# The two parts of each head trade places by transfers instead of ScalarE copies, in the rotations of a two-block transformer kernel

## The chip, the cores and the metric

One core of one Trainium2 chip. The metric is device time in microseconds (us) of the whole program; lower is better. Engines are named as in the profile: PE is TensorE's matmul, PEld its weight load, DVE VectorE, ACT ScalarE, POOL GpSimd, SP SyncE; a name with a q (ACTq, SPq, PEq) is the engine's queue, in which waits are passed and transfers are issued.

## What is computed

The reference runs a block of depth two (two attention mixers with two MLPs) over 512 tokens of width 1024, and then a second block, where the change lies. The second block applies a rotary embedding to heads of 64 channels before its attentions:

```
def apply_rope(x, cos, sin):
    half = x.shape[-1] // 2
    xf = x.astype(jnp.float32)
    x1, x2 = xf[..., :half], xf[..., half:]
    return jnp.concatenate([x1 * cos - x2 * sin, x2 * cos + x1 * sin], axis=-1).astype(x.dtype)

dq = apply_rope(...)      # four heads of two parts: differential attention
dk = apply_rope(...)
nq = apply_rope(...)      # eight query heads: compressed, selected and window attention
k_cmp = compress(apply_rope(kv(kc_), c3, s3), cmp_pe_k, cmp_k_w1, cmp_k_w2)
k_sel = apply_rope(kv(ks_), c3, s3)
k_win = apply_rope(kv(kw_), c3, s3)
```

Everything is float32. The weights come as slabs of 512 KB.

## The kernel before

**Layout.** Channels lie on the 128 partitions, tokens along the free axis (512). A slab is 128x1024 and holds, mostly, eight 128x128 weight tiles that give one 128x512 result. Each float32 product is made from two rounded parts: ScalarE rounds a slab to `w_hi` (`split`, L1052, two halves), GpSimd makes the rest `w_lo` (L456, two halves), and TensorE runs three matmuls a tile (L481 to L483). Slabs have two buffers in each of `raw`, `w_hi` and `w_lo`: slab m+2 is split when the matmuls of slab m are done, and SyncE loads the next one into `raw` (L437) when GpSimd has finished with it.

**The stage of the change.** In the second block a plan in units called halves (`E_PLAN`) strings the projections together: q, k, v for four pairs of heads, kc and vc for the compressed keys and values, ks, vs, kw, vw, four nq, the gates, and the two compression matrices w1 (slabs of sixteen narrow tiles, matmuls L848 to L850). Beside the plan run 48 steps of attention. A step s has scores on PE (L935), maxima on DVE (L1721), exponentials on ACT (`weigh`, L1154), shares on DVE (L2143 to L2148), a scaling on ACT (L1448 or L1162), a transpose on PE (`e_flip`, L944), a copy on DVE (L2134 or L2136) and the product with the values on PE (L972 or L981). Each engine takes its instructions in the program's order; nothing is rescheduled while it runs.

**A rotation.** Fifteen results are rotated, numbered n = 1 to 15 by `E_ROPE` in the order q0, k0, kc, q1, k1, q2, k2, q3, k3, ks, nq0, kw, nq1, nq2, nq3. Each has four parts:

- `e_first` on DVE: L2070 writes the bank times the signed sine to `tmp[:, n % 2]`, L2071 writes the bank times the cosine to the destination.
- `e_swaps` on ACT (L1414): four copies of 32 partitions by 512 elements, from `tmp[:, n % 2]` to `tmp[:, 2 + n % 2]`, rows r from rows r^32. From n = 3 on, it waits first for the addition of rotation n-2 (L1411).
- `e_second` on DVE: waits for `swapped`, then adds the exchanged tile to the destination (L2027) and tells PE (`rope_ready`).
- PE waits for `rope_ready` before the first scores of a pair and before the compressed scores `cs` (L904, matmuls L907).

In step s the order on ACT is: `weigh(s)`, swaps of half 2s-1, `e_half(2s)`, the scaling of step s, swaps of half 2s, `e_half(2s+1)`. On DVE it is: maxima(s), `e_half(2s)`, the copy of step s-1, the rotation's addition of half 2s-1, shares(s), `e_half(2s+1)`, the differential combination, the addition of half 2s. `e_half` on ACT holds the splits of the slabs and small work of its own (logarithm and exponential of the sub-norm, L1399 and L1400; the copies of `windows`, L1367 and L1368; `u_hi`, L1384).

ACT's queue also issued transfers before, elsewhere: the loads of x, one store of a bias table (L1212), four table loads (L1178) and half of the stores of the result (L1527).

Of the kernel before, what the change touches and what calls it, by code (L numbers as in the profile page):

```python
# [36 lines left out]
ACT = mybir.ActivationFunctionType  # L37
# [220 lines left out]
E_ROPE = {}  # L258
# [28 lines left out]
def build(nc, slabs, x_in, params_in, consts_in, pos1_in, pos2_in, rel_in, lam_in, y_out):  # L287
    n_slabs = slabs.shape[0]
    rel_rows = nc.dram_tensor("rel_rows", (8, E_LEN), F32, kind="Internal").ap()
    with ExitStack() as stack:  # L290
# [3 lines left out]
        def sem(name):  # L294
            return stack.enter_context(nc.semaphore(name))
# [25 lines left out]
        tmp = sb("tmp", [4, S])  # L321
# [73 lines left out]
        act_hi, act_lo = sem("act_hi"), sem("act_lo")  # L395
        sq_ready, acc_ready, softened = sem("sq_ready"), sem("acc_ready"), sem("softened")
        rstd_ready, squared_rstd = sem("rstd_ready"), sem("squared_rstd")
        swapped, rope_ready = sem("swapped"), sem("rope_ready")
        dve_step, act_step = sem("dve_step"), sem("act_step")
        rel_ready, masks_ready, fox_ready = sem("rel_ready"), sem("masks_ready"), sem("fox_ready")  # L400
        t_ready, y_stored = sem("t_ready"), sem("y_stored")
# [638 lines left out]
        def _(act):  # L1040
# [363 lines left out]
            def e_swaps(h):  # L1404

                for name, p, turn in ends_of(h):
                    if name in ROTATED:
                        n = E_ROPE[name, p]
                        act.wait_ge(gemm_free, taken_out[name, p])
                        if n > 2:  # L1410
                            act.wait_ge(rope_ready, n - 2)  # L1411
                        for r in range(0, P, 32):
                            o = r ^ 32
                            last = act.activation(tmp[r:r + 32, 2 + n % 2, :], tmp[o:o + 32, n % 2, :], ACT.Copy)  # L1414
                        last.then_inc(swapped, 1)

            def e_half(h):
                for name, p, turn in ends_of(h - 2):
# [113 lines left out]
        def _(dve):  # L1532
# [489 lines left out]
            def e_second(name, p):  # L2022
                if name in ROTATED:
                    n = E_ROPE[name, p]
                    dve.wait_ge(swapped, n)
                    dst = rotated(name, p)
                    dve.tensor_tensor(dst, dst, tmp[:, 2 + n % 2, :], ALU.add).then_inc(rope_ready, 1)  # L2027
                elif name == "tk":
# [26 lines left out]
            def e_first(name, p, turn):  # L2055
# [5 lines left out]
                if name == "pct" and p >= 2:  # L2061
                    dve.wait_ge(valued, e_valued(DIFF_STEPS + 8 * (p - 1)))
                if name in ROTATED and E_ROPE[name, p] > 2:
                    dve.wait_ge(swapped, E_ROPE[name, p] - 2)
                dve.wait_ge(gemm_full, c.gemm.at(1))
                c.gemm.now += 1
                if name in ROTATED:
# [3 lines left out]
                    last = dve.scalar_tensor_tensor(rotated(name, p), bank, scale, cos2[:, :], ALU.mult, ALU.mult)  # L2071
                elif name in ("v", "vc", "vs", "vw"):
                    last = dve.tensor_tensor(VT[:, :], bank, rstd[:, :], ALU.mult)
                elif name == "ng":
                    last = dve.tensor_tensor(VT[0:24, :], bank[0:24, :], rstd[0:24, :], ALU.mult)
                elif name == "b":
                    last = dve.tensor_tensor(g_b[:, p, :], bank, rstd[:, :], ALU.mult)
                elif name == "w1":
                    last = dve.tensor_copy(hs[0:CC, :], bank[0:CC, 0:256])
# [3 lines left out]
                elif name == "gt":  # L2083
                    last = dve.tensor_copy(gates[:, :, :], bank[:, 0:NB * 24])
# [307 lines left out]
```

## Time and profile before

| | us |
|---|---|
| median of 3 runs | 2106.61 |
| lowest, highest | 2105.53, 2108.70 |
| the profiled execution, its own time | 2107.49 |
| its span in the trace | 2105.70 |
| stage of the rotations in the trace | 1276 to 1560 |

The span begins with the first recorded instruction and ends with the last; 1.79 us of the profiled execution's own time lie around it. A row of a timeline reads: start, duration, engine, line, operation, destination <- sources, shape, count, and in brackets how long the engine had been idle before, with what ended it. "PEclk" is the share of full TensorE clock that was granted.

### The profile page before, as it was taken

How to read it: one execution, taken by the hardware profiler on the slowest of the kernel's cores; microseconds unless marked ns; L12 is line 12 of the kernel's file. 1: busy time of each engine (PE TensorE's matmuls, PEld its weight loads, DVE VectorE, ACT ScalarE, POOL GpSimd, SP SyncE). 2: the span in 40 equal slices, each digit the busy share in tenths (PEclk: the TensorE clock that was granted, in tenths of full speed). 3: DMA queues.
4: the chain of work that ended last, by engine and by line, in shares of the span. 5: the costliest groups of instructions: out<-in, count | busy, mean ns of one | idle time of the engine just before them, and what ended most of it. 6: DMA issues, size and time to landing. Idle time of an engine off the chain costs nothing.

```text
span 2105.7 us, 28470 instructions
## 1 busy us (share of the span) xinstructions
PE 2037.0 (97%) x9900; PEld 1604.6 (76%) x9900; DVE 967.5 (46%) x1559; ACT 902.7 (43%) x1760; POOL 870.4 (41%) x648
## 2 busy tenths in 40 slices
PE   9999999999999988899999999999999999999997
PEld 6777688888887755688888887766667888888886
DVE  6444545322255677542312255557655653323133
ACT  5444443333343654442323346656654333223234
POOL 3222354444454221254444454442113555445454
PEclk9999999999999999999999999999999999999999
DMA  4222123223222110122223322221111222323323
GB/s 156 71 71 81 59 92 101 93 97 100 93 96 90 61 41 31 41 91 100 100 91 99 100 90 80 94 97 41 41 41 62 99 92 99 100 91 100 100 90 110
DMA packets 50581, 177.88 MB, mean 84 GB/s; under 512 B 5536, under 2 KB 5800, under 8 KB 50480
## 3 DMA queue, kind: packets, MB, share of 16 engines
q1 hardware_dynamic: 48096, 172.07, 24.7%
q10 hardware_dynamic: 2384, 4.43, 0.7%
q8 instruction: 67, 1.10, 0.2%
q14 instruction: 34, 0.28, 0.0%
HBM read 174.36 MB, written 2.12 MB: 84 GB/s over the span
## 4 chain that ended last, share of the span: by engine, by line
issue 47%; PE 31%; POOL 19%; DVE 2%; POOLq 1%; ACT 0%; DVEq 0%; ACTq 0%
POOL w_lo L456 19%; PE gemm_banks L481 9%; PE gemm_banks L482 9%; PE gemm_banks L483 9%; PE score_banks L935 1%; PE out_bank L981 1%; PE score_banks L944 1%; DVE turned L2136 1%; POOLq L450 0%; POOLq L455 0%; PE gemm_banks L907 0%; DVE score_banks L1721 0%; DVE x L2232 0%; PE out_bank L972 0%; ACT tmp L1414 0%
## 5 line engine op out<-in xcount | busy, mean ns | idle before, releaser
L456 POOL TENSOR_TENSOR w_lo<-raw,w_hi 128x512 fp32r<-128x512 f32 x644 | 870.2, 1373 | 1218.1 <-ACT w_hi L1052 1218.0
L1052 ACT ACTIVATE w_hi<-raw 128x512 fp32r<-128x512 f32 x644 | 370.9, 623 | 824.5 <-PE gemm_banks L483 809.4
L481 PE MATMUL gemm_banks<-h_hi,w_hi 128*128 128x512 f32 x1512 | 611.3, 404 | 3.1 <-POOL w_lo L456 2.9
L483 PE MATMUL gemm_banks<-h_hi,w_lo 128*128 128x512 f32 x1512 | 590.5, 391 | 0.0
L482 PE MATMUL gemm_banks<-h_lo,w_hi 128*128 128x512 f32 x1512 | 589.7, 390 | 0.0
L481 PEld LDWEIGHTS gemm_banks<-h_hi,w_hi 128*128 128x128 f32 x1512 | 283.0, 187 | 93.8 <-issue 34.7
L481 PE MATMUL gemm_banks<-u_hi,w_hi 128*128 128x512 f32 x848 | 330.3, 390 | 4.2 <-POOL w_lo L456 2.9
L483 PEld LDWEIGHTS gemm_banks<-h_hi,w_lo 128*128 128x128 f32 x1512 | 282.8, 187 | 62.1
L483 PE MATMUL gemm_banks<-u_hi,w_lo 128*128 128x512 f32 x848 | 329.9, 389 | 0.0
L482 PE MATMUL gemm_banks<-u_lo,w_hi 128*128 128x512 f32 x848 | 329.9, 389 | 0.0
L482 PEld LDWEIGHTS gemm_banks<-h_lo,w_hi 128*128 128x128 f32 x1512 | 283.4, 187 | 56.3 <-issue 2.6
L1620 DVE TENSOR_TENSOR x<-gemm_banks,x 128x512 f32<-128x512 f32 x112 | 77.4, 691 | 308.0 <-PE gemm_banks L483 305.7
L481 PEld LDWEIGHTS gemm_banks<-u_hi,w_hi 128*128 128x128 f32 x848 | 159.2, 188 | 38.7 <-issue 3.7
L483 PEld LDWEIGHTS gemm_banks<-u_hi,w_lo 128*128 128x128 f32 x848 | 159.2, 188 | 33.1
L482 PEld LDWEIGHTS gemm_banks<-u_lo,w_hi 128*128 128x128 f32 x848 | 159.2, 188 | 32.9
L1821 DVE TENSOR_TENSOR u_lo<-tmp,u_hi 128x512 fp32r<-128x512 f32 x86 | 108.4, 1260 | 125.6 <-ACT u_hi L1250 108.6
L1154 ACT ACTIVATE probs<-score_banks,top 128x128 f32<-128x128 f32 (+3 forms) x192 | 99.6, 523 | 141.7 <-DVE top L1721 140.0
L1162 ACT ACTIVATE probs<-probs,share 128x128 f32<-128x128 f32 (+3 forms) x160 | 81.1, 554 | 71.3 <-DVE share L1743 36.0
L1556 DVE TENSOR_TENSOR tmp<-gemm_banks,rstd 128x512 f32<-128x512 f32 x52 | 36.0, 692 | 141.0 <-PE gemm_banks L483 139.7
L1813 DVE SCALAR_TENSOR_TENSOR tmp<-gemm_banks,rstd 128x512 f32<-128x512 f32 x64 | 44.3, 692 | 121.4 <-PE gemm_banks L483 118.7
L1575 DVE TENSOR_TENSOR acc<-acc,sq 128x512 f32<-128x512 f32 x51 | 70.9, 1390 | 10.1 <-ACT sq L1070 9.3
L1721 DVE CUSTOM_DVE_ANT_0 score_banks<-score_banks,sin 128x128 f32<-128x128 f32 (+3 forms) x96 | 45.4, 514 | 39.0 <-PE score_banks L935 38.9
(316 smaller groups left out, 1889.8 us busy)
## 6 DMA issues: line engine op xcount, KB each, us to landing
raw<-slabs SPq DMA_DIRECT2D x322, 512.0 KB, 3.3
table<-rel_rows ACTq DMA_DIRECT2D x4, 512.0 KB, 3.8
x<-x_t SPq DMA_DIRECT2D x4, 256.0 KB, 6.7
x<-x_t ACTq DMA_DIRECT2D x4, 256.0 KB, 6.9
cos<-pos SPq DMA_DIRECT2D x2, 256.0 KB, 10.4
y_t<-x SPq DMA_DIRECT2D x2, 256.0 KB, 2.9
y_t<-x ACTq DMA_DIRECT2D x2, 256.0 KB, 2.7
y_t<-x SPq DMA_DIRECT2D x1, 512.0 KB, 2.8
```

Of the source, the lines that this page charges most:

```text
L456: pool.tensor_tensor(w_lo[:, j, part], raw[:, j, part], w_hi[:, j, part].bitcast(F32), ALU.subtract).then_inc(slab_split, 1)
L481: pe.matmul(out, high, rhs_hi, start=first, stop=False)
L482: pe.matmul(out, high, rhs_lo, start=False, stop=False)
L483: return pe.matmul(out, low, rhs_hi, start=False, stop=last)
L1052: act.activation(w_hi[:, m % 2, part], raw[:, m % 2, part], ACT.Copy).then_inc(slab_hi, 1)
L1154: act.activation(probs[:, b, head, 0:w], SC[:, 2 * b + head, 0:w], ACT.Exp, bias=top[:, b, head:head + 1], scale=-1.0, accum_out=mass[:, b ...
L1162: act.activation(probs[:, b, head, 0:w], probs[:, b, head, 0:w], ACT.Copy, scale=share[:, b, head:head + 1]).then_inc(evened, 1)
L1575: dve.tensor_tensor(sums[:, :], sums[:, :], sq[:, c.acc.slot, :], ALU.add).then_inc(acc_ready, 1)
L1620: dve.tensor_tensor(x[:, j, :], bank, x[:, j, :], ALU.add).then_inc(gemm_free, 1)
L1721: last = dve.tensor_tensor_reduce(z, z, masks[head], -1.0, 3e38, ALU.add, ALU.min, top[:, b, head:head + 1])
L1813: dve.scalar_tensor_tensor(tmp[:, s, :], result(), 0.0, rstd[:, :], ALU.max, ALU.mult).then_inc(gemm_free, 1)
L1821: dve.tensor_tensor(u_lo[:, j, :], tmp[:, 2 + s, :], u_hi[:, j, :].bitcast(F32), ALU.subtract).then_inc(act_lo, 1)
```

## The change

The four copies of a rotation become four transfers of 64 KB, from the same rows of `tmp` to the same rows, issued on ACT's queue. Each adds 16 to a semaphore; there are now two semaphores, one for odd n and one for even n, and who waits for rotation n waits for 64 times the number of rotations of that parity so far. The waits ahead of the exchange (for `e_first`, and for the addition of rotation n-2) are the same.

```
-        swapped, rope_ready = sem("swapped"), sem("rope_ready")
+        swapped, rope_ready = [sem("swapped0"), sem("swapped1")], sem("rope_ready")
...
                         for r in range(0, P, 32):
                             o = r ^ 32
-                            last = act.activation(tmp[r:r + 32, 2 + n % 2, :], tmp[o:o + 32, n % 2, :], ACT.Copy)
-                        last.then_inc(swapped, 1)
+                            act.dma_start(tmp[r:r + 32, 2 + n % 2, :], tmp[o:o + 32, n % 2, :]).then_inc(swapped[n % 2], 16)
...
                     n = E_ROPE[name, p]
-                    dve.wait_ge(swapped, n)
+                    dve.wait_ge(swapped[n % 2], 64 * ((n + 1) // 2))
...
                 if name in ROTATED and E_ROPE[name, p] > 2:
-                    dve.wait_ge(swapped, E_ROPE[name, p] - 2)
+                    n = E_ROPE[name, p] - 2
+                    dve.wait_ge(swapped[n % 2], 64 * ((n + 1) // 2))
```

## Rows read from the trace of the kernel before

**Rows 1.** The page: busy time of each engine over the span, its share, instructions.

```profile
PE 2037.0 (97%) x9900; PEld 1604.6 (76%) x9900; DVE 967.5 (46%) x1559; ACT 902.7 (43%) x1760; POOL 870.4 (41%) x648
```

**Rows 2.** Windows: the stage, and eight us in it; last clock, DMA share, GB/s.

```profile
1276.00:1560.00 284.00, 261.82 (x1456) 194.12 (x1456) 173.39 (x433) 173.42 (x391) 94.13 (x69) 0.97 0.19 64
...
1392.00:1400.00 8.00, 6.44 (x32) 6.04 (x33) 5.17 (x11) 5.59 (x13) 6.53 (x5) 0.57 0.31 88
```

**Rows 3.** Waits, 1265 to 1560: us in total, times, longest.

```profile
PE gemm_banks L848 <- POOL w_lo L456: 7.7, 6, 3.4
...
PE gemm_banks L907 <- issue: 4.4, 2, 2.4
...
ACT w_hi L1052 <- DMA raw<-slabs: 9.7, 5, 3.1
```

**Rows 4.** The copies' line: duration in ns min/median/max, first and last start.

```profile
L1414 ACT ACTIVATE tmp<-tmp x60: 625/629/633, 1277.9 to 1543.1; 32x512 f32<-32x512 f32 x60
```

**Rows 5.** Timeline at L1212's issue, early in the kernel.

```profile
45.83 0.54 ACTq L1212 DMA_DIRECT2D rel_rows<-table  x1
...
47.54 0.19 ACT L1210 ACTIVATE small<-small 128x2 f32<-128x2 f32 x1
```

**Rows 6.** ACT's issues: ns of one; then us to landing, of L1178 and of L1527.

```profile
L1178 ACTq DMA_DIRECT2D table<-rel_rows x4: 366/372/408, 92.5 to 189.9; - x4
...
DMA to landing us min/median/max: 3.6/3.8/5.3
DMA to landing us min/median/max: 2.3/3.1/3.2
```

**Rows 7.** The page: a slab's transfer, KB each, median us to landing.

```profile
raw<-slabs SPq DMA_DIRECT2D x322, 512.0 KB, 3.3
```

**Rows 8.** Timeline at rotation 14, with the wait of its line L1411.

```profile
L1411 ACTq EVENT_SEMAPHORE  x1: 17/17/17, 1498.4 to 1498.4; - x1
...
1499.62 2.54 ACT L1414 ACTIVATE tmp<-tmp 32x512 f32<-32x512 f32 x4
...
1502.19 0.69 DVE L2027 TENSOR_TENSOR QT<-QT,tmp 128x512 f32<-128x512 f32 x1 [3.14 <-ACT tmp L1414]
...
1502.98 1.08 PE L907 MATMUL gemm_banks<-kcmp,QT 128*128 128x64 f32 x8 [2.37 <-issue]
```

**Rows 9.** Timeline at rotations 13 and 15: the addition, and PE behind it.

```profile
1457.97 0.69 DVE L2027 TENSOR_TENSOR QT<-QT,tmp 128x512 f32<-128x512 f32 x1 [2.06 <-ACT tmp L1414]
...
1459.93 0.66 PE L944 MATMUL score_banks<-consts,probs 128*128 128x128 f32 x4 [1.56 <-ACT probs L1162]
...
1543.73 0.69 DVE L2027 TENSOR_TENSOR QT<-QT,tmp 128x512 f32<-128x512 f32 x1 [3.76 <-ACT tmp L1414]
...
1544.53 1.08 PE L907 MATMUL gemm_banks<-kcmp,QT 128*128 128x64 f32 x8 [2.04 <-issue]
```

**Rows 10.** Timeline at rotation 10.

```profile
1387.71 2.55 ACT L1414 ACTIVATE tmp<-tmp 32x512 f32<-32x512 f32 x4
...
1391.48 1.13 ACT L1052 ACTIVATE w_hi<-raw 128x512 fp32r<-128x512 f32 x2
...
1393.54 0.47 PE L848 MATMUL gemm_banks<-w_hi,blk_hi 128*62 128x256 f32 x1 [3.44 <-POOL w_lo L456]
```

**Rows 11.** Timeline at rotations 1, 2.

```profile
1277.89 2.56 ACT L1414 ACTIVATE tmp<-tmp 32x512 f32<-32x512 f32 x4 [3.72 <-DVE QT L2071]
...
1281.65 2.56 ACT L1414 ACTIVATE tmp<-tmp 32x512 f32<-32x512 f32 x4
1282.61 0.47 PE L481 MATMUL gemm_banks<-h_hi,w_hi 128*128 128x512 f32 x1 [0.44 <-POOL w_lo L456]
...
1285.58 0.66 PE L880 MATMUL gemm_banks<-consts,VT 128*128 128x128 f32 x4 [1.35 <-DVE VT L2073]
```

**Rows 12.** Timeline behind rotations 3 and 5.

```profile
1303.72 0.47 PE L481 MATMUL gemm_banks<-h_hi,w_hi 128*128 128x512 f32 x1 [0.85 <-POOL w_lo L456]
...
1321.37 0.33 PE L848 MATMUL gemm_banks<-w_hi,blk_hi 128*62 128x256 f32 x1 [1.05 <-POOL w_lo L456]
```

## The prediction

> **What bounds the kernel now.** I read the page first. PE is busy 97% of the span and no other engine reaches half [rows 1], so a change on ACT is worth what it takes out of, or puts into, PE's idle time, and nothing more. The rotations lie between 1276 and 1560. The windows say that PE is busy there for 261.8 of 284 us, so 22 us of idle time are in reach, and that the granted clock is 0.97 on average but 0.57 in one stretch of 8 us behind the longest gap [rows 2]. ACT is busy 61% of the stage: it is not the bound, but everything on it is in order. The waits then say what PE stood for: 7.7 us for slabs whose second part GpSimd had not made, and 4.4 us before L907 [rows 3]. L907 is the compressed score, which needs a rotated query, so those 4.4 us belong to rotations. Last I read the timeline at each of the 15 rotations: where the copies begin and end, when DVE adds, and whether PE has a gap behind it. Those that have one are rotations 13, 14, 15 directly, 10 and 5 through a slab split that stands behind the copies on ACT, 1 and 2 in both ways, 3 through the windows of kc.
>
> **What is removed.** 60 copies of 0.629 us [rows 4]; four in a row take 2.55 us, 38 us of ACT in all. DVE's addition starts when the fourth ends: 11 of the 15 additions stand waiting for it.
>
> **What is added.** Sixty issues on ACT's queue, and a landing. Two questions decide: when does the first issue start, and how long is it until the fourth transfer has landed?
>
> *Start.* An issue need not wait for ACT's datapath. L1212 was issued at 45.83, while L1210, which stands ahead of it in the program, ran at 47.54 [rows 5]: the queue was at least 1.7 us ahead. At the rotations the wait record of L1411 shows where the queue is. At rotation 14 it passes at 1498.4, at the start of the exponentials, and the copies start at 1499.62 [rows 8]: 1.2 us of head start H that copies cannot use and issues can. The 12 rotations from 4 on have such a record, H 0.4 to 1.9 us; it is 1.2 at rotation 10, 1.0 at 13, 1.1 at 15. Rotations 1 and 3 have none, since the copies there wait for DVE itself.
>
> *Issue.* L1178 took 0.372 us for 128 rows, L1212 0.54 us [rows 5, 6]. Nothing shows an issue of 32 rows. I take 0.37 and keep 0.54 for the range; an issue of fewer rows could be cheaper, but 8 rows were not. Four take 1.5 us of ACT's queue, so what stands behind the copies can start 1.05 us earlier, and H more where ACT had work.
>
> *Landing.* From issue to landing a transfer of 256 KB out of this memory took 2.3 us at least (3.1 the median of three) [rows 6], a slab of 512 KB 3.3 [rows 7]. The trace has none of 64 KB, and none that stays on the chip. From above I bound it by 3.3. From below: 3.3 - 2.3 is 1.0 us for 256 KB more, so 192 KB less than 256 would be 0.75 us less, 1.55. I take 2.0, nearer to the smaller transfer. The fourth then lands 3 x 0.37 + 2.0 = 3.11 us after the first issue, where the copies ended H + 2.55 us after that moment. A rotation is thus later by 0.56 - H: later by 0.56 without a head start, earlier by 0.6 with H = 1.2.
>
> The Trainium skill (DMA: Bandwidth & Descriptors, section Anatomy of one DMA) splits a transfer's time into about 2.0 us that do not shrink with size, mostly the receipt of the write, and the bytes at 436 GB/s, fitted for GpSimd's path. By that 64 KB would be an estimated 2.15 us and each rotation 0.15 us later than I have it, the whole sum about 0.6 us smaller; the 256 KB store at 2.3 [rows 6] is below the 2.6 that the fit gives, so the trace puts the fixed part somewhat lower.
>
> **The sum, place by place, as PE sees it.**
>
> *Rotation 14.* The issue starts at 1498.4, lands at 1501.5; the addition was at 1502.19 and PE's L907 directly behind it after 2.37 us idle [rows 8]. -0.7. *Rotation 15*: the queue is there at 1540.0, landing 1543.1 against 1543.73, PE idle 2.04 behind [rows 9]. -0.6. *Rotation 13*: 1454.4 plus 3.11 is 1457.5 against 1457.97; shares, ACT's L1162 and the transpose stand behind the addition, PE idle 1.56 [rows 9]. -0.5. Together -1.8. With 1.55 us for the landing -3.1, with 3.3 +2.1, with issues of 0.54 1.5 worse than either.
>
> *Rotation 10.* Copies 1387.71 to 1390.26, then L1399 and L1400 (0.6 us each), then the split of a w1 slab at 1391.48, GpSimd, and PE after 3.44 us idle, the longest gap of the stage [rows 10]. PE had left that buffer and the raw slab had landed before the copies began. Issues start at 1386.5 and end at 1388.0, so all that follows is 2.3 us earlier. -2.3. The next slab, whose load waits for GpSimd, moves with it and no further. Without head start -1.1, at most the whole gap, -3.4.
>
> *Rotations 1 and 2.* ACT leaves rotation 1 at 1279.4 instead of 1280.45, so the split behind it, and the 0.44 us that PE waits at 1282.61, go. Rotation 2 could issue right behind that split's dispatch, about 1279.5, and land at 1282.6; the copies ended at 1284.21, and DVE's L2073, queued behind that addition, was what PE waited 1.35 us for [rows 11]. Both gaps sum to 1.8; I take -1.6, since v itself ends at 1282.2. With landing 3.3, -0.9.
>
> *Rotation 3.* No head start: the addition is 0.5 us later; behind it stand four window copies, DVE's L2000, ACT's L1372, then a split for which PE waits 0.85 us [rows 12]. +0.5 (0 to +1.8).
>
> *Rotation 5.* The split behind it comes 1.7 us earlier, and PE waits 1.05 us for it [rows 12]. But the split after that one waits for exponentials behind DVE's addition, unmoved, and the w1 slabs follow one another by their loads: most is lost again. -0.3 (0 to -1.05).
>
> *The other seven* (4, 6 to 9, 11, 12): 0. Projections of eight tiles cover them; PE has no gap within 5 us behind any of them. In the worst case, 3.3 us to land, the addition is 1.5 us later than now, less than the 2 to 3.5 us that DVE waits for banks anyway in these steps.
>
> *New waits.* DVE stands at the addition as before, with shares and maxima behind it; that is counted above. Its wait ahead of L2070 is for a transfer two rotations back: 0. *Other transfers*: 60 x 64 KB is 3.8 MB over 284 us, which move 64 GB/s with the rings busy 19% [rows 2]. A slab in flight could come up to a us later; the five splits that waited for a slab, 9.7 us [rows 3], are all in the w1 stretches, some 8 us behind the nearest rotation: 0.
>
> Sum: -1.8 - 2.3 - 1.6 + 0.5 - 0.3 = -5.5. The profiled span 2105.7 becomes 2100.2, its own time 2107.49 becomes 2102.0. That execution stood 0.9 above the median of the runs, so against the median of 2106.6 I forecast **2101.1 us**.
>
> **The rivals.**
>
> *The issue has no head start* (an issue waits until the exponentials are done). Against it: rows 5. Then 13, 14, 15 are +0.56 each, rotation 10 is -1.1, 1 and 2 -1.3, 3 +0.5, 5 -0.2: -0.4, 2106. A landing of 3.0 us with head start comes to the same region: for 13 to 15 together +1.3, and -2.3, -1.1, +1.5, -0.3, which is -0.9. Chance of this region, no change that can be measured (under 0.2%, 4.2 us, of this kernel), 0.28.
>
> *The transfers are slow because slabs share the rings.* One mechanism: slab loads start at 1499.27 and 1541.38, within the issues of rotations 14 and 15. For it: L1178 needed up to 5.3 us where its median is 3.8 [rows 6]. A landing of 4.7 us gives 13 to 15 +2.2 each (0.56 - H + 2.7), 3 +3.2, 1 and 2 and 5 0, and rotation 10 -1.3 once its addition is the later: about +8.5, 2115. It decides from a landing of about 4.0 us on, where the sum passes +4.2. Against it: a slab needs the rings for two of its 3.3 us and the rotation is ahead of it. Chance 0.12.
>
> *The clock comes back too.* At 1392 to 1400 the granted clock was 0.57, that is mostly 1.2 GHz, after PE had idled 3.44 us [rows 2, 10]; 4 us behind rotation 13 and 4 behind 15 look the same at 0.59 and 0.57. Half clock there costs PE about 3.4, 1.6 and 1.7 us, the first mostly covered by GpSimd's halves. If gaps of 2.04 and 1.56 us shrink by a third the drops may not come: 3 us more, 2098; with the low landing 2095. Chance 0.15. The Trainium skill (TensorE: Matmul & The Clock Gate, section HAM oscillation) says likewise that idle gaps turn the clock down; rotation 14's gap of 2.37 us was not followed by one, so which gap pays is open.
>
> **How the numbers follow.** Forecast 0.45, clock too 0.15, no change 0.28, slow landing 0.12. Faster by over 0.2%: 0.45 + 0.15 - 0.02 for the forecast's own edge = 0.58; within: 0.30; slower: 0.12. Range: down to 2095.5, which takes in most of the clock case, up to 2108.0, which takes in the landing at 3.3 us (+2.1 - 2.3 - 0.9 + 1.8 = +0.7, 2107.3); the forecast's own range is 2098.5 to 2103.5.
>
> **What the profile will show.** Right: 60 ACTq issues of about 0.37 us on the changed line; landings near 2 us; the first issue of rotation 14 at the start of L1154, not at its end; DVE's wait at that addition 2.4 instead of 3.14 us; the gap before L848 behind rotation 10 near 1.1 us; ACT 38 us less busy. Wrong: landings of 3.5 us and more, or stretches where a slab and a rotation delay each other; issues spaced by 0.54; gaps before L907 over 2.4 us; a new stretch of half clock where none was.

## The result, and the profile after

The changed kernel takes 2129.07 us (median of 5 runs, 2124.96 to 2130.38) against 2106.61 us (5 runs): ratio 1.0103, 95% interval 1.0089 to 1.0116. The change makes the kernel 22 us slower; the forecast was 5.5 us faster, with a range that ended at 2108.0. The profiled execution has a span of 2128.6 us and an own time of 2130.38 us. The lines of code behind L1414 stand one lower than before: DVE's addition is L2026.

First the page, then two windows, with rotations 11 to 13, and 14 and 15 (columns as in [rows 2]).

```profile
PE 2043.5 (96%) x9900; PEld 1608.7 (76%) x9900; DVE 969.7 (46%) x1559; ACT 866.2 (41%) x1700; POOL 872.0 (41%) x648
```

```profile
1400.00:1500.00 100.00, 90.32 (x496) 64.88 (x495) 62.46 (x159) 46.83 (x117) 27.56 (x20) 0.92 0.21 66
1500.00:1600.00 100.00, 87.76 (x545) 62.73 (x543) 54.93 (x164) 48.84 (x133) 17.67 (x14) 0.93 0.13 40
```

ACT is 36.5 us less busy, as said, and it bought nothing. PE's idle time rose from 2105.7 - 2037.0 = 68.7 us [rows 1] to 2128.6 - 2043.5 = 85.1, by 16.4; the same 9900 matmuls took 6.5 us more. Together 22.9, the growth of the span. The slower matmuls go with the clock: from 1400 on the granted clock is 0.92 and 0.93, where the kernel before had 0.98 in both stretches, and within the stage alone the same 1456 matmuls take 270.5 us instead of 261.8. (PE's busy time over the whole span is not fixed: with the copies and the written-out loop, e6 below, it is 2029.2, so a few us of clock come and go outside the change.)

The issues, by the changed line (ns of one, min/median/max), with their landings:

```profile
L1414 ACTq DMA_DIRECT2D tmp<-tmp x60: 513/612/1740, 1278.7 to 1560.9; - x60
...
DMA to landing us min/median/max: 1.9/2.4/4.9
```

The waits from 1265 to 1585 (us in total, times, longest), to be read against [rows 3]:

```profile
PE gemm_banks L907 <- issue: 8.3, 2, 4.4
...
PE gemm_banks L880 <- DVE VT L2073: 5.5, 2, 3.2
```

L907, the compressed score, waits 8.3 us where it waited 4.4. L880 waits twice, 5.5 us; the second time is new. Now the timeline at rotation 14, the counterpart of [rows 8]:

```profile
1513.10 0.58 ACT L1154 ACTIVATE probs<-score_banks,top 128x384 f32<-128x384 f32 x1 [1.35 <-DVE top L1720]
...
1513.16 0.51 ACTq L1414 DMA_DIRECT2D tmp<-tmp  x1
...
1513.70 0.62 ACTq L1414 DMA_DIRECT2D tmp<-tmp  x1
...
1514.02 0.33 SPq L437 DMA_DIRECT2D raw<-slabs  x1
...
1514.35 1.25 ACTq L1414 DMA_DIRECT2D tmp<-tmp  x2
...
1518.45 0.69 DVE L2026 TENSOR_TENSOR QT<-QT,tmp 128x512 f32<-128x512 f32 x1 [4.65 <-DMA tmp<-tmp]
...
1519.24 1.94 PE L907 MATMUL gemm_banks<-kcmp,QT 128*128 128x64 f32 x8 [3.89 <-issue]
```

Four things are in these lines. The first transfer is issued 0.06 us behind the start of the exponentials: the head start is real. The issues follow one another every 0.54 to 0.65 us, so the fourth starts 1.8 to 1.9 us behind the first. A slab's load starts in the middle of them, and the addition is 5.29 us behind the first issue. And the eight small matmuls take 1.94 us where they took 1.08, at a lower clock. Rotation 13, where the slab's load starts only when all four transfers have been issued, and rotation 15, where it starts in between (before: [rows 9]):

```profile
1471.47 0.69 DVE L2026 TENSOR_TENSOR QT<-QT,tmp 128x512 f32<-128x512 f32 x1 [2.36 <-DMA tmp<-tmp]
...
1473.43 0.81 PE L944 MATMUL score_banks<-consts,probs 128*128 128x128 f32 x4 [1.87 <-ACT probs L1162]
...
1559.02 0.52 ACTq L1414 DMA_DIRECT2D tmp<-tmp  x1
...
1565.01 0.69 DVE L2026 TENSOR_TENSOR QT<-QT,tmp 128x512 f32<-128x512 f32 x1 [6.08 <-DMA tmp<-tmp]
...
1565.80 1.81 PE L907 MATMUL gemm_banks<-kcmp,QT 128*128 128x64 f32 x8 [4.37 <-issue]
```

Rotation 13's first issue is at 1467.60, so its addition is 3.87 us behind it; rotation 15's is 5.99 behind. Rotation 12, where L880 had no gap before:

```profile
1435.24 3.57 ACTq L1414 DMA_DIRECT2D tmp<-tmp  x4
...
1436.17 0.33 SPq L437 DMA_DIRECT2D raw<-slabs  x1
...
1438.86 0.63 ACT L1384 ACTIVATE u_hi<-sq_e 128x512 fp32r<-128x512 f32 x1 [3.06 <-issue]
...
1441.08 0.69 DVE L2026 TENSOR_TENSOR k_win<-k_win,tmp 128x512 f32<-128x512 f32 x1 [4.02 <-DMA tmp<-tmp]
...
1445.54 0.66 PE L880 MATMUL gemm_banks<-consts,VT 128*128 128x128 f32 x4 [3.16 <-DVE VT L2073]
```

Here one issue took 1.74 us, the longest of the 60, the four held ACT's queue for 3.57 us, and ACT itself stood idle behind them. In the 4 us from 1435 on the trace has, beside the slab and the four transfers, one packet of a further queue, which the page calls instruction (2.1% of 16 engines over 4 us is 1.35 us of one engine):

```profile
q8 instruction: 1, 0.02, 2.1%
```

It is taken up again under e5. Rotations 3, 2 and 10 ([rows 12, 11, 10] have their counterparts):

```profile
1293.72 3.10 ACTq L1414 DMA_DIRECT2D tmp<-tmp  x4
...
1295.73 0.33 SPq L437 DMA_DIRECT2D raw<-slabs  x1
...
1300.44 0.69 DVE L2026 TENSOR_TENSOR sq_e<-sq_e,tmp 128x512 f32<-128x512 f32 x1 [6.11 <-DMA tmp<-tmp]
...
1306.69 0.33 PE L944 MATMUL score_banks<-consts,probs 128*128 128x128 f32 x1 [2.03 <-DVE probs L2155]
...
1309.74 0.58 PE L481 MATMUL gemm_banks<-h_hi,w_hi 128*128 128x512 f32 x1 [2.72 <-DVE QT L2071]
```

```profile
1287.47 0.66 PE L880 MATMUL gemm_banks<-consts,VT 128*128 128x128 f32 x4 [2.38 <-DVE VT L2073]
...
1398.62 0.43 PE L848 MATMUL gemm_banks<-w_hi,blk_hi 128*62 128x256 f32 x1 [1.76 <-POOL w_lo L456]
```

**Where the lateness grows.** The additions' starts in the two traces give a running account. Ahead of the first rotation the changed kernel's execution already stood 0.8 us later (L2071 at 1278.00 against 1277.18), which is no work of the change. By rotation 6 (1358.43 against 1351.67) it is 6.8 us late, by rotation 11 8.3 (1433.47 against 1425.13), rotation 12 11.6 (1441.08 against 1429.48), 13 13.5, 14 16.3, 15 21.3, at the end 22.9. So rotations 1 to 5 cost 6.0 us (nearly all at rotation 3), 6 to 11 1.5, 12 3.3, 13 1.9, 14 2.8, 15 5.0, and 1.6 come behind it (each figure holds the lateness of the addition itself, whether PE felt it or not). PE's own gaps, summed place by place, grow by 1.0 us at rotations 1 and 2, 3.9 at 3, 1.1 at 10, 3.2 at 12, 0.3 at 13, 1.5 at 14 and 2.3 at 15: 13.3 of the 16.4.

### The profile page after: what moved, and what is told of

It is laid out like the page before. It is cut to its first block, busy times and chain, and to the rows that moved or that the text cites. A ratio compares the mean times of both kernels' runs of the same rounds, so it can differ in the third digit from the quotient of the medians.

```text
span 2128.6 us, 28470 instructions
## 1 busy us (share of the span) xinstructions
PE 2043.5 (96%) x9900; PEld 1608.7 (76%) x9900; DVE 969.7 (46%) x1559; ACT 866.2 (41%) x1700; POOL 872.0 (41%) x648
## 4 chain that ended last, share of the span: by engine, by line
issue 47%; PE 30%; POOL 19%; DVE 2%; POOLq 1%; ACT 0%; DMA 0%; ACTq 0%; DVEq 0%
POOL w_lo L456 19%; PE gemm_banks L481 9%; PE gemm_banks L483 9%; PE gemm_banks L482 9%; PE score_banks L935 1%; PE out_bank L981 1%; PE score_banks L944 1%; DVE turned L2136 1%; POOLq L450 0%; POOLq L455 0%; PE gemm_banks L907 0%; DMA tmp<-tmp 0%; DVE score_banks L1720 0%; DVE x L2232 0%; ACTq L1414 0%
## 5 line engine op out<-in xcount | busy, mean ns | idle before, releaser
L1154 ACT ACTIVATE probs<-score_banks,top 128x128 f32<-128x128 f32 (+3 forms) x192 | 99.6, 524 | 163.7 <-DVE top L1720 158.6
```

What stands on the lines that cost most here:

```text
L1154: act.activation(probs[:, b, head, 0:w], SC[:, 2 * b + head, 0:w], ACT.Exp, bias=top[:, b, head:head + 1], scale=-1.0, accum_out=mass[:, b ...
```

## The experiments

Two theories stood at the start. A: the exchange is late, and ACT's queue is held, because an issue costs 0.6 us and a slab in flight stretches the landings. B: it is the bytes of the transfers in the rings and the memory, whoever waits for them. All ratios below are against the kernel before, run beside each experiment. It stood at 2106.0 to 2106.6 us each time, so the medians can be compared with one another to about 1 us. Three kernels leave something out: e2 and e13 exchange rows 64 apart, not 32, and e11 exchanges a quarter of the columns.

| run | median us | ratio, 95% interval |
|---|---|---|
| e1 half copies | 2105.24 | 0.9996 (0.9985 to 1.0006) |
| e2 two issues | 2111.17 | 1.0027 (1.0015 to 1.0038) |
| e3 copies and four unused transfers | 2108.12 | 1.0006 (0.9997 to 1.0016) |
| e4 issued by SyncE | 2101.89 | 0.9976 (0.9966 to 0.9986) |
| e5 slab held back | 2116.01 | 1.0040 (1.0026 to 1.0054) |
| e6 copies, loop written out | 2107.84 | 1.0005 (0.9997 to 1.0014) |
| e7 six copies | 2125.90 | 1.0084 (1.0067 to 1.0100) |
| e8 eight copies | 2144.60 | 1.0180 (1.0165 to 1.0195) |
| e9 two copies behind | 2114.43 | 1.0043 (1.0029 to 1.0057) |
| e10 SyncE, two unused ahead | 2116.07 | 1.0045 (1.0031 to 1.0059) |
| e11 a quarter of the width | 2125.61 | 1.0088 (1.0073 to 1.0103) |
| e12 half copies, half SyncE | 2097.82 | 0.9961 (0.9947 to 0.9975) |
| e13 two issues, slab held back | 2103.14 | 0.9982 (0.9973 to 0.9991) |
| e14 two queues | 2111.16 | 1.0024 (1.0015 to 1.0034) |

### e1: half of the exchange by transfers

Lines against the kernel before; DVE waits for both semaphores.

```
+                        for r in (0, 32):
+                            o = r ^ 32
+                            act.dma_start(tmp[r:r + 32, 2 + n % 2, :], tmp[o:o + 32, n % 2, :]).then_inc(swapped[n % 2], 16)
+                        for r in (64, 96):
...
                             last = act.activation(tmp[r:r + 32, 2 + n % 2, :], tmp[o:o + 32, n % 2, :], ACT.Copy)
```

> Rows 0 to 63 of each exchange by two transfers, rows 64 to 127 by two copies behind them. Theory A (the count of issues: four cost 2.5 us of ACT's queue, 0.64 us apart, instead of the 1.5 us of the prediction, so that the fourth transfer starts 1.9 us late): the second transfer lands 0.64 + 2.0 us after the first issue, the copies end 1.28 + 1.27 us after it, so each addition comes some 1.2 us sooner than in the changed kernel and the loss falls from 22 us to under 5: 2104 to 2112. Rival B (landings stretched by slabs that share the rings, from 2.0 to 3 to 5 us): the last landing still falls in a slab's time, additions wait for it, 2115 to 2122.

Measured: 2105.2 us, no difference. At rotation 14 ACT's issues start 1.2 us ahead of its copies and the addition waits 2.01 us, not 3.14. At rotations 3, 9, 10 and 12 the addition still stands 4.2 to 4.9 us behind the first issue. What the one place gives the other takes.

### e2: two issues of 64 rows in place of four of 32

```
-                        for r in range(0, P, 32):
-                            o = r ^ 32
-                            act.dma_start(tmp[r:r + 32, ...], tmp[o:o + 32, ...]).then_inc(swapped[n % 2], 16)
+                        for r in (0, 64):
+                            o = r ^ 64
+                            act.dma_start(tmp[r:r + 64, ...], tmp[o:o + 64, ...]).then_inc(swapped[n % 2], 16)
```

> Two transfers of 64 rows each (rows r from r^64, so the wrong rows are exchanged, but as many bytes): same bytes, half the issues. Theory A: the last transfer starts 0.64 instead of 1.9 us behind the first, ACT's queue is free after 1.3 instead of 2.5 us; additions 1.2 us sooner, 2105 to 2112. Rival B: bytes and the sharing with slabs are unchanged, 2118 to 2126.

Measured: 2111.2, so half of the issues take back 17.9 us of 22. The same bytes move. Its issues take as long as those of half the size:

```profile
L1414 ACTq DMA_DIRECT2D tmp<-tmp x30: 468/510/631, 1277.4 to 1546.4; - x30
...
DMA to landing us min/median/max: 2.2/2.7/4.7
```

ACT's queue is held 1.12 us in each rotation instead of 2.44, and rotation 13's addition is 2.87 us behind the first issue instead of 3.87.

### e3: the copies stay, and four transfers that nobody reads are added

```
                         last.then_inc(swapped, 1)
+                        if n > 1:
+                            act.wait_ge(spare_landed, 64 * (n - 1))
+                        for r in range(0, P, 32):
+                            act.dma_start(spare[r:r + 32, :], consts[r:r + 32, 0:480]).then_inc(spare_landed, 16)
```

> The kernel before, with its four copies, plus four transfers of 60 KB a rotation that nobody but the next rotation's issue waits for. The issues can run while the copies run in ACT's datapath. Theory A with the new wait as the cause (additions late by issue and landing): little, 2106 to 2111. Rival C (ACT's queue being occupied, or the extra bytes in the rings making slabs late, is what costs, whoever waits): over 2114.

Measured: 2108.1, no difference: 3.7 MB more through the rings cost nothing that can be measured, and theory B falls. The trace adds a limit to what this run says of the queue: at rotation 10 the issues were sent from 1387.76 on and the copies, ahead of them in the program, ran from 1388.83, so the first two lay beside ACT's exponentials and the others beside the copies: they held ACT hardly at all, and the run says nothing of what issues cost that ACT has to wait for.

### e4 and e6: the transfers issued by SyncE's queue, and its control

```
             for m in range(190, 232):
                 for n, taken_at in before_load.get(m, ()):
+                    sp.wait_ge(gemm_free, taken_at)
+                    if n > 2:
+                        sp.wait_ge(rope_ready, n - 2)
+                    for r in range(0, P, 32):
+                        o = r ^ 32
+                        sp.dma_start(tmp[r:r + 32, 2 + n % 2, :], tmp[o:o + 32, n % 2, :]).then_inc(swapped[n % 2], 16)
                 load(m // 2, m % 2)
```

> The same four transfers, issued by SP's queue between slab loads (its loop is written out for slabs 190 to 231) as soon as DVE has written the sine part, not in ACT's turn. ACT has neither copies nor issues. Theory A: at rotations 13 to 15 DVE is done 1 to 3 us before ACT's turn, so the last landing is 3.9 us behind that and additions come at about the time of before; ACT's splits come 2.5 us sooner: 2100 to 2108. Rival B: slabs, now right behind on the same queue, stretch landings to 4 us and are late themselves: 2112 to 2125.

> The kernel before, with its four copies, and only SyncE's loop over the slabs written out for slabs 190 to 231, as in the version whose transfers were issued by SyncE's queue (2101.9). It changes nothing of the rotations. Theory A, that version's gain of 5 us came from the transfers being issued by a queue that has nothing else to do: this one is at the time before, 2104.5 to 2108.5. Theory B, the gain came from the written-out loop (its loads without the loop's registers and branches): about 2102.

Measured: 2101.9, faster than the kernel before; the loop written out with the copies kept is at 2107.8, so the gain is the transfers'. Rotation 14 in e4:

```profile
1496.16 2.42 SPq L2238 DMA_DIRECT2D tmp<-tmp  x4
...
1499.02 0.33 SPq L2223 DMA_DIRECT2D raw<-slabs  x1
...
1499.99 0.69 DVE L2000 TENSOR_TENSOR QT<-QT,tmp 128x512 f32<-128x512 f32 x1 [1.03 <-DMA tmp<-tmp]
...
1500.78 1.08 PE L887 MATMUL gemm_banks<-kcmp,QT 128*128 128x64 f32 x8 [0.27 <-issue]
```

The issues are 0.6 us apart here too, and the addition is 3.83 us behind the first. But they need not wait for ACT's turn; the slab stands behind them in the same queue; and PE's gap before the compressed score is 0.27 us where it was 2.37.

### e5: the slab held back until the transfers have landed

```
             for m in range(190, 232):
+                for n in before_load.get(m, ()):
+                    sp.wait_ge(swapped[n % 2], 64 * ((n + 1) // 2))
                 load(m // 2, m % 2)
```

> The changed kernel with one addition: in the stage of the rotations SyncE's queue does not start the load of the slab that is due beside a rotation until that rotation's four transfers have landed (its loop is written out for slabs 190 to 231). Theory A, the transfers of rotations 3, 5, 10, 12, 14 and 15 landed 1 to 3 us late because a slab of 512 KB was in flight beside them: in the changed kernel the addition started 6.72, 3.97, 6.04, 5.84, 5.29 and 5.99 us behind the first issue, and 3.87 at rotation 13 where no slab was. Then it is 3.8 to 4.1 us everywhere, landings are 1.9 to 2.2 us, and the time falls by some 6 to 14 us, to 2115 to 2123 (the issues, 0.62 us apart, still cost the rest). Theory B, the landings vary for another reason (64 KB out of 32 partitions, or the fourth transfer behind the first three): the additions stay 5 to 6.7 us behind and the time is 2127 or, as the slabs now come later too, more.

Measured: 2116.0, 13 us of the 22 back, though the slabs now come later. Rotation 14, to be read against the changed kernel's above:

```profile
1507.01 0.52 ACTq L1432 DMA_DIRECT2D tmp<-tmp  x1
...
1510.87 0.33 SPq L441 DMA_DIRECT2D raw<-slabs  x1
...
1510.87 0.69 DVE L2044 TENSOR_TENSOR QT<-QT,tmp 128x512 f32<-128x512 f32 x1 [3.23 <-DMA tmp<-tmp]
...
1511.66 1.08 PE L925 MATMUL gemm_banks<-kcmp,QT 128*128 128x64 f32 x8 [2.46 <-issue]
```

The addition is 3.86 us behind the first issue instead of 5.29, PE's gap 2.46 instead of 3.89, and the matmuls are back at 1.08 us. Rotations 12 to 15 add 2.5 us to the lateness instead of 13.0 (7.8 at rotation 11, 10.3 at 15). At rotations 3, 9 and 12 the addition is still 4.78, 4.53 and 4.64 us behind the first issue. At 3 and 9 no slab explains it: the loads around them are issued 7.3 and 3.9 us ahead of the first issue and after the last landing. What lies there instead is one packet of the instruction queue. At rotation 9, the four issues, and then the DMA view of 1382 to 1386, in which no slab's packet stands:

```profile
1381.68 3.11 ACTq L1432 DMA_DIRECT2D tmp<-tmp  x4
...
q8 instruction: 1, 0.02, 1.8%
```

The third of these issues took 1.28 us. Rotations 14 and 15, with neither a slab nor such a packet beside their transfers, have four issues in 2.44 us and the addition at 3.86. So there are two disturbances. The slab's load is the larger; it is what e5 takes away at 14 and 15.

### e7, e8 and e9: lateness without any transfer

```
+                        if n > 1:
+                            act.wait_ge(spare_done, n - 1)
+                        for r in (0, 32):
+                            o = r ^ 32
+                            last = act.activation(spare[r:r + 32, :], tmp[o:o + 32, n % 2, 0:480], ACT.Copy)
+                        last.then_inc(spare_done, 1)
                         for r in range(0, P, 32):
                             o = r ^ 32
                             last = act.activation(tmp[r:r + 32, 2 + n % 2, :], tmp[o:o + 32, n % 2, :], ACT.Copy)
                         last.then_inc(swapped, 1)
```

e8 has four such copies; e9 has the added lines behind `last.then_inc(swapped, 1)`.

> The kernel before with two copies more in each rotation, ahead of its four, into a tile that nobody reads (480 of 512 columns; they leave the result as it is). No transfers. The exchange ends 1.26 us later and ACT is held 1.26 us longer, which is what the changed kernel's undisturbed rotation shows for the exchange (3.87 us instead of 2.58 from start to addition). It calibrates what lateness alone costs. Theory A, the time follows the lateness as PE sees it at the few places that have a gap behind them, once per place (rotations 13, 14, 15, 10, 1, 2, 3): 1.26 x 7 = 9 us, 2113 to 2119, clock included. Theory B, nothing but these gaps and no clock: 2110 to 2112. Theory C, lateness is covered and the transfers harm in another way (rings, ports): under 2109.

> As the one with two copies more, but with four more: the exchange ends 2.5 us later and ACT is held 2.5 us longer, 5.1 us from start to addition, about what the disturbed rotations of the changed kernel show (5.0 to 6.7). If the time follows the lateness (theory A) it is 2124 to 2134, at or above the changed kernel; if it grows faster than the lateness, because places that were covered come to the front, over 2134. If lateness is mostly covered (theory C), under 2115.

> The two unused copies of the run with six copies (which cost 19.3 us, 1.27 us for each of 15 rotations), now behind the four real ones: ACT is held 1.26 us longer as there, but the exchange ends where it did. It tells a late addition from a held ACT. Theory A, what costs is that ACT is held (slab splits, exponentials and casts behind the copies): 2120 to 2126, as with the copies ahead. Theory B, what costs is the late addition on DVE, and ACT behind it has slack: 2106 to 2110. Half each: 2113 to 2117.

Measured: 2125.9, 2144.6 and 2114.4. Both expectations of e7 were too low: it costs 19.3 us, and e8 38.0, twice that. Two copies hold ACT 1.24 us, so 1 us in each of the 15 rotations is worth 15.6 us of the kernel. That is an average, and it does not mean that nothing is covered: from the addition of rotation 6 to that of rotation 11 e7 falls behind by only 1.4 us (8.1 to 9.5) for five times 1.24 us, and from there to the end by 9.7 for four times. Most of rotations 7 to 11 is covered; the last four pay about double. e9 splits the 19.3: a held ACT costs 8.0 us and the late addition, if the two simply add, the other 11.3. Each is seen where it should be. The late addition: at rotation 14 e7's gap is 3.61 us and e9's is the old 2.37. The held ACT: behind rotation 10 e9 has a gap of 4.66 us instead of 3.44. First e7, then e9:

```profile
1518.65 1.72 PE L909 MATMUL gemm_banks<-kcmp,QT 128*128 128x64 f32 x7 [3.61 <-issue]
```

```profile
1398.27 0.47 PE L850 MATMUL gemm_banks<-w_hi,blk_hi 128*62 128x256 f32 x1 [4.66 <-POOL w_lo L458]
...
1507.70 1.08 PE L909 MATMUL gemm_banks<-kcmp,QT 128*128 128x64 f32 x8 [2.37 <-issue]
```

### e10: the late addition alone, with transfers

```
+                    if n > 1:
+                        sp.wait_ge(spare_landed, 32 * (n - 1))
+                    for r in (0, 32):
+                        sp.dma_start(spare[r:r + 32, :], consts[r:r + 32, 0:480]).then_inc(spare_landed, 16)
                     for r in range(0, P, 32):
```

> The version whose four transfers are issued by SyncE's queue (2101.9, ACT neither copies nor issues), with two transfers of 60 KB that nobody reads issued ahead of the four: the exchange lands 1.2 us later and ACT is not held at all. Theory A (a held ACT costs, a late addition does not): 2101 to 2105. Theory B (a late addition costs, 1.2 us for each rotation whose addition stands waiting, 10 of 15): 2110 to 2118. Slabs come 1.2 us later too, which the trace must show to be harmless.

Measured: 2116.1, 14.2 us more than e4 for two issues more on a queue that does not touch ACT. At rotation 14 the two take 1.19 us, from 1506.50 to the first exchange at 1507.69. The late addition is a cost of its own. Slabs come later too, so 14.2 is its upper bound; e9 puts it at 11.3 for 1.24 us.

### e11: a quarter of the bytes

```
-    act.dma_start(tmp[r:r + 32, 2 + n % 2, :], tmp[o:o + 32, n % 2, :]).then_inc(swapped[n % 2], 16)
+    act.dma_start(tmp[r:r + 32, 2 + n % 2, 0:128], tmp[o:o + 32, n % 2, 0:128]).then_inc(swapped[n % 2], 16)
```

> The changed kernel with transfers of 128 of the 512 columns (16 KB in place of 64): three quarters of the exchange are left out, the issues stay as they are, four on ACT's queue. Theory A, the transfers are late because their packets stand in the rings behind those of a slab of 512 KB: a quarter of the bytes stands behind the same slab, so landings of 3 us and more stay where a slab is in flight, undisturbed ones fall by 0.1 to 0.4 us, and the time is 2122 to 2127. Theory B, their own bytes are what shares the rings: landings are under 2.3 us throughout and the time is 2115 to 2119, as with the slab held back (2116.0).

Measured: 2125.6.

```profile
L1414 ACTq DMA_DIRECT2D tmp<-tmp x60: 514/612/1268, 1278.1 to 1557.9; - x60
...
DMA to landing us min/median/max: 1.7/2.0/4.2
```

An issue costs the same 612 ns for a quarter of the bytes. Undisturbed, 48 KB less are worth 0.2 us (1.7 against 1.9; rotation 13's addition at 3.64 against 3.87). Beside a slab the addition is still 4.75 us behind the first issue at rotation 14, 5.07 at 15 and 6.09 at 12. So the lateness comes with the slab's load and hardly with the transfers' own volume. The Trainium skill (DMA: Bandwidth & Descriptors, section Queues, rings and completion order) says that SyncE and ScalarE each own one ring on each of the same 16 engines, and that an engine drains a whole packet of one ring before it turns to the next. That agrees with e5 and e11; that the size of a slab's packets is what sets the added 1.4 to 2.1 us no run here shows.

### e12: half copies, half SyncE

In e4's loop `for r in (0, 32)`; ACT copies the rows of `r in (64, 96)` as in e1.

> Rows 0 to 63 exchanged by two transfers issued by SyncE's queue ahead of the slab, rows 64 to 127 by two copies on ACT: ACT held 1.27 us in place of 2.55, and only two issues, so the last transfer lands 0.6 + 2.0 = 2.6 us behind its start in place of 3.8. Theory: if both the held ACT and the late addition cost, this is the best of all, 2094 to 2100; if only the addition does, about 2097 to 2102; if only the held ACT does, it is above the version without copies, 2103 to 2106.

Measured: 2097.8, the best of all, 8.6 us under the kernel before on the same chip. Rotation 14:

```profile
1493.84 1.26 ACT L1396 ACTIVATE tmp<-tmp 32x512 f32<-32x512 f32 x2
...
1495.20 0.69 DVE L2010 TENSOR_TENSOR QT<-QT,tmp 128x512 f32<-128x512 f32 x1 [1.92 <-ACT tmp L1396]
```

SyncE's two transfers are issued from 1490.51 on, so the addition waits only for the second copy, and PE's gap behind it is 1.16 us. Both costs are cut: ACT is held 1.26 us instead of 2.55, and the addition comes sooner.

### e13 and e14: what is left of the 22 us

e13 is e5 with e2's loop. e14 is e12 with ACT's two copies made transfers:

```
                         for r in (64, 96):
                             o = r ^ 32
-                            last = act.activation(tmp[r:r + 32, 2 + n % 2, :], tmp[o:o + 32, n % 2, :], ACT.Copy)
-                        last.then_inc(copied, 1)
+                            act.dma_start(tmp[r:r + 32, 2 + n % 2, :], tmp[o:o + 32, n % 2, :]).then_inc(copied[n % 2], 16)
```

> Two edits together: the slab is held back until the rotation's transfers have landed (alone: 2116.0), and the exchange goes by two issues of 64 rows in place of four of 32 (alone: 2111.2; the halves are 64 rows apart, so the wrong rows are exchanged, with the same bytes). Theory A, the 9.4 us that are left over the time before once no slab is in flight are the price of issues 0.6 us apart, which hold ACT for 2.45 us and start the fourth transfer 1.9 us late: then the addition is 2.9 us behind the first issue everywhere, ACT is held 1.1 us, and the time is 2100 to 2106, below before. Theory B, part of it is something else (holding the slab back itself costs, or the clock): 2107 to 2113.

> The four transfers of 32 rows, issued by two queues side by side: rows 0 to 63 by SyncE's ahead of the slab, rows 64 to 127 by ACT's. ACT's queue is held 1.1 us, the last transfer starts 0.6 us behind the first of its queue. Theory A (issue spacing is the price, and a slab that is queued behind two of the transfers mostly keeps out of their way): additions 2.6 us behind ACT's first issue, 2095 to 2101, as the run with half copies (2097.8). Theory B, ACT's two transfers still meet the slab that SyncE's queue starts right behind its own two, and land at 3 us and more: 2102 to 2112.

Measured: e13 2103.1, below the time before. The held slab alone gives 13.1 us, and two issues in place of four then give 12.9 more: 26, over the 22 that were lost. The edits overlap, since two issues alone give 17.9, and the held slab then 8.0 more. So each of the two causes has a price between two bounds, 12.9 to 17.9 us for the count of issues and 8.0 to 13.1 us for the slabs, and together they are enough for the whole loss. Rotation 14 in e13:

```profile
1498.77 0.47 ACTq L1432 DMA_DIRECT2D tmp<-tmp  x1
...
1502.44 1.07 PE L925 MATMUL gemm_banks<-kcmp,QT 128*128 128x64 f32 x8 [1.75 <-issue]
```

e14 is at 2111.2, theory B's region: two queues side by side halve the issues of each, but ACT's two meet the slab that SyncE's queue starts in the meantime.

```profile
1503.11 0.51 ACTq L1396 DMA_DIRECT2D tmp<-tmp  x1
...
1503.52 0.33 SPq L2233 DMA_DIRECT2D raw<-slabs  x1
...
1503.65 0.78 ACTq L1396 DMA_DIRECT2D tmp<-tmp  x1
...
1507.30 0.69 DVE L2009 TENSOR_TENSOR QT<-QT,tmp 128x512 f32<-128x512 f32 x1 [3.83 <-DMA tmp<-tmp]
```

The slab is issued 0.4 us behind the first of ACT's transfers; the addition comes 3.65 us behind the second of ACT's. At rotations 13 and 15 the load starts 2.05 and 1.15 us behind ACT's first issue, when both of its transfers are out, and there the addition is 2.7 us behind.

## Why the prediction was wrong

**Right: the landing.** "I take 2.0": undisturbed landings are 1.9 to 2.1 us.

**Right: the head start.** Rotation 14's first issue is 0.06 us behind the start of L1154. The rival without head start falls.

**Right: the formula for 13, 14 and 15.** It said that PE's gap moves by what the addition moves against the moment at which the queue arrives. Rotation 13: 3.57 us before (1454.4 to 1457.97) and 3.87 after, +0.30, the gap 1.56 to 1.87. Rotation 14: 3.79 and 5.29, +1.50, the gap 2.37 to 3.89. Rotation 15: 3.73 and 5.99, +2.26, the gap 2.04 to 4.37. The frame held to a tenth of a us; what was put into it did not.

**Wrong, the first step: the issue, "I take 0.37 and keep 0.54 for the range".** An issue takes 0.51 us for the first and 0.61 for each that follows, 0.03 apart: the fourth starts 1.8 to 1.9 us behind the first, not 1.11, and ACT's queue is free after 2.44 us, not 1.5. That is as long as the four copies had held it, so "what stands behind the copies can start 1.05 us earlier" was worth nothing but H. Neither bound held it. The rows that I took were of transfers between memory and chip, each issued alone; the nearest row, 0.54, was nearest to the first of a series only. Two issues in place of four are worth 12.9 to 17.9 us (e13, e2). That is more than the step itself, for two issues hold the queue 1.12 us, less than the 1.5 that I forecast for four. My error of 0.94 us in the time that ACT's queue is held is 0.7 of the 1.32 us by which the two loops differ, so the step is worth an estimated 9 to 13 us.

**Wrong, the second step: "Other transfers: 0".** I weighed what the exchange does to the slabs and found nothing, which was right (e3). What the slabs do to the exchange I put at a rival with 0.12. Loads of slabs start 0.9 and 1.3 us behind the first issue at rotations 14 and 15, 0.9 at 12 and 2.0 at 3. The addition is then 5.3 to 6.7 us behind the first issue instead of 3.9 (at 3 and 12 a packet of the instruction queue lies there too, which I had not foreseen; in e5, with the slab held back, 4.8 and 4.6 are left). Price 8.0 to 13.1 us. The rival had the mechanism and rotations 3, 14 and 15; it also counted 13, where the load came too late to matter, and left out 12. "It decides from a landing of about 4.0 us on" was computed with the issue at 0.37. At rotation 14 no landing was over 3.6 us and it decided all the same.

**Wrong, the third step: "The other seven: 0. Projections of eight tiles cover them".** For 6 to 9 and 11 it held (rotations 7 to 11 add 1.5 us together, and in e7 1.4). At rotation 12 a gap of 3.16 us appeared. "PE has no gap within 5 us behind" says that there is cover, not how much. I bounded the addition at 1.5 us later; it started 5.84 us behind the first issue, and ACT was held 1 us longer than by copies.

**Wrong in size.** These follow from the steps above. Rotation 10: -2.3 forecast; the gap of 3.44 us became four of 1.76, 1.32, 0.77 and, before L944, 0.64, 4.5 in all. Rotation 3: +0.5 forecast, the addition 4.1 us later (6.72 us from start to addition instead of 2.59), and two gaps of 2.03 and 2.72 us where 0.85 was. Rotations 1 and 2: -1.6 forecast, the gap before L880 grew from 1.35 to 2.38, and that of 0.44 stayed (0.46). Rotation 5: -0.3 forecast; the five gaps before L848 behind it went from 4.30 to 4.44 us.

**The clock, with the sign turned.** The rival said that shorter gaps might spare the drops. The gaps grew and there are more drops: in the 12 us behind the gap of rotation 14 the granted clock is 0.72 where it was 1.00 before, behind rotation 15 0.72 against 0.86; in a stretch with 0.72 part of the time is at 2.4 GHz and the rest at 1.2, half of full. Rows of the changed kernel, 12 us each, from a little before PE resumes:

```profile
1518.00:1530.00 12.00, 10.63 (x55) 8.53 (x56) 7.61 (x23) 4.20 (x10) 0.00 (x0) 0.72 0.00 0
1564.00:1576.00 12.00, 10.04 (x44) 6.94 (x44) 6.98 (x21) 4.22 (x11) 0.00 (x0) 0.72 0.00 0
```

In e13, with gaps of 1.75 and 1.24 us, both stretches are at 1.00. So a longer gap is paid twice: 16.4 us of idle time and 6.5 us of slower matmuls here. Which gap brings the clock down, the runs don't settle: e5's rotation 14, with 2.46 us, is followed by 0.86 and its rotation 15, with 2.24, by 0.72, while the kernel before with 2.37 is followed by 1.00 and with 2.04 by 0.86.

**What stays open.** Why an issue of 32 or 64 rows inside the chip takes 0.61 us in a series, while one of a slab takes 0.33 (SyncE, 128 rows of 4 KB) and a store of 256 KB 0.36. And why a few issues take over 1 us. SyncE issuing a slab at the same time does not explain them: at rotation 14 of the changed kernel the slab's issue (1514.02, 0.33 us) lies beside an issue of ACT's that took 0.62. In the traces of the eleven kernels that issue such small transfers, thirteen issues took 1.09 to 1.74 us. Beside every one of them lay a packet of the instruction queue, and each ended 0.3 to 0.4 us after that packet did; seven of them had no slab's issue beside them. At rotation 12 of e11 the slab is issued 0.92 us behind the first transfer as in the changed kernel, the packet came only after the issues, and the four took 2.44 us, not 3.57. That is where the long issues stand in every trace, not how they come about: no run moves or removes the packet. The Trainium skill (Perfetto Trace Analysis, section DMA Instruction — HWDGE) says that the block that makes the descriptors is shared by sequencers and that the profiled time of an issue includes the wait for its lock. Such a wait would look like this, but no run here shows who would hold the lock.

## What to carry to other kernels

- Cost a series of issues by count, not by bytes, and look for a row of a *series*: four issues of 0.61 us held ScalarE's queue as long as the four copies of 0.63 us that they replaced, and two issues of double size were 12.9 to 17.9 us cheaper over 15 rotations. Where the transfers are short, issue them from a queue that is idle and put the next large load behind them in that same queue (2101.9), or split the work between copies and such a queue (2097.8).
- Ask in both directions: what does my transfer do to the others, and what do they do to mine? A 64 KB transfer that somebody waits for is the one that loses to a 512 KB load.
- Before trusting "covered", make the thing longer by a known amount and see where the lateness grows: two more copies in the kernel before show that one us in each rotation is worth 15.6 us in all, little of it at rotations 7 to 11 and about double at the last four.

## What the runs showed of the hardware

- Transfers inside the chip land in 1.7 us (16 KB), 1.9 (64 KB) and 2.2 (128 KB) at least; with the load of a 512 KB slab started beside them, a 64 KB transfer takes up to 4.2 and a 16 KB one up to 3.6 at rotation 15, and 4.9 and 4.2 where a packet of the instruction queue lies there too.
- An issue of such a transfer takes 0.51 us first and 0.61 then on ScalarE's queue (0.47 and 0.61 for 64 rows), the same for a quarter of the bytes, and 0.51 and 0.6 on SyncE's.
- ScalarE's queue sends issues that stand behind copies in the program before the copies run (e3: 1.07 us ahead at rotation 10).
- A transfer's issue beside which a packet of the instruction queue is under way can take 1.09 to 1.74 us instead of 0.61 (13 cases in eleven traces, 7 of them with no slab issued beside it).
